# RWKV-7 decays of a head pair: from token-major products to a channel-major product and a scan on VectorE

## What is computed

```
w_log = -softplus(-(w0 + tanh(wl) @ w2)) - 0.5       # wl: 96 low-rank columns of each token
decay = exp(-exp(w_log))                             # one number for each token and channel
S_t   = S_{t-1} * decay_t + (rank-one terms)         # for each token of a sequence, in order
```

## Time and profile before

| | |
|---|---|
| median of 3 runs | 1846.82 us (1845.8 to 1849.24) |
| span of the profiled execution | 1844.8 us, 1.0 us under the fastest run's device time |
| granted TensorE clock, mean | 0.996 |
| TensorE matmul busy | 1811.2 us (98%), weight loads 1733.0 us (94%) |
| VectorE busy | 1132.4 us (61%) |
| ScalarE busy | 729.2 us (40%) |
| chain that ended last | TensorE 94%, VectorE 3%, ScalarE 1%, DMA 1% |
| length of a loop pass | 47.4 us |

### The profile page before, as it was taken

One profiled execution on the slowest core, in us unless ns is written; L12 is line 12 of the kernel. 1 busy time (PEld: TensorE's weight loads), 2 busy tenths in 40 slices (PEclk: granted clock), 3 DMA queues, 4 the chain that ended last, 5 costly groups with the idle time before them and its releaser, 6 DMA issues.

```text
span 1844.8 us, 41091 instructions
## 1 busy us (share of the span) xinstructions
PE 1811.2 (98%) x16688; PEld 1733.0 (94%) x16688; DVE 1132.4 (61%) x2000; ACT 729.2 (40%) x1013; POOL 51.6 (3%) x100
## 2 busy tenths in 40 slices
PE   7999999999999999999999999999999999999997
PEld 6999788888888888899999999999999999999997
DVE  6645675467777777766556666666666665434444
ACT  5433434344444444433444333333333333333332
POOL 0600000000000000000000000000000000000000
PEclk9999999999999999999999999999999999999999
DMA  6644334333333332355446444544445445544443
GB/s 238 223 160 158 108 115 160 119 128 109 107 107 107 107 102 91 130 199 166 167 170 219 160 162 161 177 160 159 161 163 176 159 159 184 188 163 166 161 167 129
DMA packets 50832, 283.52 MB, mean 154 GB/s; under 512 B 7104, under 2 KB 12288, under 8 KB 24656
## 3 DMA queue, kind: packets, MB, share of 16 engines
q1 hardware_dynamic: 43488, 260.80, 41.6%
q10 hardware_dynamic: 3216, 12.82, 1.8%
q0 software_dynamic: 4064, 8.98, 1.5%
HBM read 274.31 MB, written 8.27 MB: 153 GB/s over the span
## 4 chain that ended last, share of the span: by engine, by line
PE 94%; DVE 3%; ACT 1%; DMA 1%; issue 1%; SPq 0%; ACTq 0%; DVEq 0%
PE bank L596 29%; PE bank L598 27%; PE bank L597 27%; PE bank L925 1%; PE bank L960 1%; DVE w_lo L544 1%; PE bank L612 1%; PE bank L1025 0%; PE bank L947 0%; DVE max L1813 0%; PE bank L577 0%; PE bank L725 0%; PE bank L882 0%; PE bank L701 0%; PE bank L791 0%
## 5 line engine op out<-in xcount | busy, mean ns | idle before, releaser
L596 PE MATMUL bank<-x_split,w_lo 128*128 128x288 f32 x2944 | 899.3, 305 | 7.1 <-DVE w_lo L544 6.9
L597 PE MATMUL bank<-x_split,w_hi 128*128 128x288 f32 x2944 | 869.2, 295 | 0.0
L598 PE MATMUL bank<-x_split,w_hi 128*128 128x288 f32 x2944 | 867.0, 294 | 0.0
L560 ACT ACTIVATE w_hi<-w_raw 128x2048 fp32r<-128x2048 f32 (+1 forms) x262 | 468.8, 1790 | 590.4 <-PE bank L598 571.7
L544 DVE TENSOR_TENSOR w_lo<-w_raw,w_hi 128x2048 fp32r<-128x2048 f32 (+1 forms) x238 | 503.6, 2116 | 283.8 <-ACT w_hi L560 283.5
L596 PEld LDWEIGHTS bank<-x_split,w_lo 128*128 128x128 f32 x2944 | 552.4, 188 | 32.1 <-issue 13.6
L597 PEld LDWEIGHTS bank<-x_split,w_hi 128*128 128x128 f32 x2944 | 553.8, 188 | 3.1 <-issue 0.7
L598 PEld LDWEIGHTS bank<-x_split,w_hi 128*128 128x128 f32 x2944 | 554.9, 188 | 0.0
L596 PE MATMUL bank<-act_split,w_lo 128*128 128x288 f32 x704 | 208.6, 296 | 0.0
L597 PE MATMUL bank<-act_split,w_hi 128*128 128x288 f32 x704 | 207.7, 295 | 0.0
L598 PE MATMUL bank<-act_split,w_hi 128*128 128x288 f32 x704 | 207.0, 294 | 0.0
(11 more groups left out here) (384 smaller groups left out, 1499.9 us busy)
## 6 DMA issues: line engine op xcount, KB each, us to landing
w_raw<-in_w_up SPq DMA_DIRECT2D x88, 1024.0 KB, 4.8
w_raw<-in_w_in SPq DMA_DIRECT2D x48, 1024.0 KB, 5.0
w_raw<-in_w_down SPq DMA_DIRECT2D x64, 704.0 KB, 4.1
w_raw<-in_w_gate SPq DMA_DIRECT2D x32, 1024.0 KB, 4.9
w_raw<-in_w_p SPq DMA_DIRECT2D x16, 1024.0 KB, 4.9
w_raw<-in_w_o SPq DMA_DIRECT2D x16, 1024.0 KB, 4.8
x_raw<-in_x SPq DMA_DIRECT2D x4, 576.0 KB, 5.7
h<-in_x ACTq DMA_DIRECT2D x1, 2304.0 KB, 11.1
```

The costliest lines, as they stand in the source:

```text
L560: actv(WHI[:, slot, 0:kt], WRAW[:, slot, 0:kt], ACT.Copy).then_inc(sem("w_hi"), 3 if isinstance(n, int) and n == 2 else 1)
L596: mm(out, wl, hi, start=first and k == ks[0], stop=False, skip_group_check=True)
L597: mm(out, w, lo, start=False, stop=False, skip_group_check=True)
L598: ins = mm(out, w, hi, start=False, stop=last and k == ks[-1], skip_group_check=True)
```

## The change

On TensorE the three token-major products for z become one product with the 128 channels stationary and all 288 tokens moving, so that z has the channels on the partitions at once; `log_decay` (three products and its waits) is gone from TensorE. On ScalarE tanh and the addition of 1 write the tile `log_decays`, 300 columns, in which a zero column stands ahead of each chunk. On VectorE one instruction, `tensor_tensor_scan` over 300 columns, makes the running sums in place: it multiplies the running value by a constant tile that is 0 at the head of each chunk and 1 elsewhere, and adds the next column. It stands between the first two quarters of a split and `k_mixed`. The exps read this tile from SBUF and carry the scale that the triangular constant held. The constants grow from 144 to 104 columns in one tile and from 130 to 300 in the other, 130 columns more together. VectorE clears the new tile once, ahead of the loop.

```diff
-    tri = np.zeros((P, 2, CH + 1))
-    tri[:, :, 1:] = ((blk(CH) & upi) * (0.5 * DECAY_SCALE)).reshape(P, 2, CH)
-    c["tri"] = tri.reshape(P, -1)
+    keep = np.ones((P, DEC))
+    keep[:, 0:NCH * (CH + 1):CH + 1] = 0.0
+    keep[:, NCH * (CH + 1):DEC:DS + 1] = 0.0
+    c["scan_keep"] = keep
...
-    LDT = m("decay_tok", [P, 3, P])
+    LDS = m("log_decays", [P, DEC])
+    ldv = LDS[:, 0:NCH * (CH + 1)].rearrange("p (c f) -> p c f", f=CH + 1)
+    ldv_s = LDS[:, NCH * (CH + 1):DEC].rearrange("p (b f) -> p b f", f=DS + 1)
...
                 lw = COLS[:, T_LW]
-                for tt in range(2):
-                    mm(BK[2][:, tt * P:(tt + 1) * P], lw[0:97, tt * P:(tt + 1) * P], LORA[0:97, 0, :], start=True, stop=True)
-                mm(BK[2][0:NS, 2 * P:3 * P], lw[0:97, SEQ:N], LORA[0:97, 0, :], start=True,
-                   stop=True).then_inc(sem("z_mm"), 1)
+                mm(BK[2][:, 0:N], LORA[0:LORA_W + 1, 0, :], lw[0:LORA_W + 1, 0:N], start=True, stop=True).then_inc(sem("z_mm"), 1)
...
-            def log_decay(v):
-
-                pe.wait_ge(sem("decay_tok"), v)
-                pe.wait_ge(sem("g_sb"), v)
-                for tt in range(2):
-                    w = 2 * (CH + 1)
-                    mm(BK[7][:, tt * w:(tt + 1) * w], LDT[:, tt, :], tri, start=True, stop=True)
-                mm(BK[7][:, NCH * (CH + 1):DEC], LDT[0:NS, 2, :], tri_s, start=True, stop=True).then_inc(sem("log_decay"), 1)
...
                 mm(BK[5][:, 0:N], head_ones, YQ[:], start=True, stop=True).then_inc(sem("y_var"), 1)
-                if not last:
-                    log_decay(it + 2)
                 fill(6)
...
             fill_cols(FILL_DECAY)
-            log_decay(1)
             fill_cols(FILL_BONUS)
...
                 act.wait_ge(sem("z_mm"), v)
-                actv(LDT[:, 0:2, :].rearrange("p t f -> p (t f)"), BK[2][:, 0:2 * P], ACT.Tanh, scale=0.5)
-                actv(LDT[0:NS, 2, :], BK[2][0:NS, 2 * P:3 * P], ACT.Tanh, scale=0.5).then_inc(sem("z_tanh"), 1)
+                actv(ldv[:, :, 1:], BK[2][:, 0:SEQ].rearrange("p (c f) -> p c f", f=CH), ACT.Tanh, scale=0.5)
+                actv(ldv_s[:, :, 1:], by_request(BK[2][:, SEQ:N]), ACT.Tanh, scale=0.5).then_inc(sem("z_tanh"), 1)
...
-                actv(LDT[:, 0:2, :], LDT[:, 0:2, :], ACT.Copy, bias=1.0)
-                actv(LDT[0:NS, 2, :], LDT[0:NS, 2, :], ACT.Copy, bias=1.0).then_inc(sem("decay_tok"), 1)
+                actv(ldv[:, :, 1:], ldv[:, :, 1:], ACT.Copy, bias=1.0)
+                actv(ldv_s[:, :, 1:], ldv_s[:, :, 1:], ACT.Copy, bias=1.0).then_inc(sem("decay_tok"), 1)
...
                 act.wait_ge(sem("log_decay"), v)
-                actv(PEXP[:, 0, :], BK[7][:, 0:DEC], ACT.Exp)
-                actv(PEXP[:, 1, :], BK[7][:, 0:DEC], ACT.Exp, scale=-1.0).then_inc(sem("decay"), 1)
+                actv(PEXP[:, 0, :], LDS[:], ACT.Exp, scale=0.5 * DECAY_SCALE)
+                actv(PEXP[:, 1, :], LDS[:], ACT.Exp, scale=-0.5 * DECAY_SCALE).then_inc(sem("decay"), 1)
...
+            V.memset(LDS[:], 0.0)
...
+            def log_decay(v):
+
+                dve.wait_ge(sem("decay_tok"), v)
+                V.tensor_tensor_scan(LDS[:], scan_keep, LDS[:], 0.0, ALU.mult, ALU.add).then_inc(sem("log_decay"), 1)
...
                 for part in range(2):
                     split_part(dve, n + 3, 1, part)
                 if not last:
+                    log_decay(it + 2)
                     k_mixed(it + 2)
...
             kk_max(1)
+            log_decay(1)
             k_mixed(1)
```

More of the change, by code:

```diff
@@ L114, in constants @@
     b4 = blk(DS)
-    small = np.zeros((P, 3 * NS + DB * (DS + 1) + DB))
+    small = np.zeros((P, 3 * NS + DB))
     both = slice(0, 2 * NS)
@@ L119, in constants @@
     small[s, 2 * NS:3 * NS] = (b4 & low)[s, s]
-    for b in range(DB):
-        small[s, 3 * NS + 5 * b + 1:3 * NS + 5 * b + 5] = (b4 & upi)[s, DS * b:DS * b + DS] * (0.5 * DECAY_SCALE)
-    small[both, 3 * NS + 5 * DB:] = np.arange(2 * NS)[:, None] % NS // DS == np.arange(DB)[None, :]
+    small[both, 3 * NS:] = np.arange(2 * NS)[:, None] % NS // DS == np.arange(DB)[None, :]
     c["small"] = small
@@ L430, in build @@
     mean_ones = MEANS[:]
-    tri = cst("tri")
+    scan_keep = cst("scan_keep")
     eye_ch, m_ab, eye_bl, m16u, m32u = (cst(x) for x in ("eye_ch", "m_ab", "eye_bl", "m16u", "m32u"))
@@ L435, in build @@
     ms_ab, ms_l = small[:, 0:2 * NS], small[:, 2 * NS:3 * NS]
-    tri_s = small[:, 3 * NS:3 * NS + 5 * DB]
-    ms_req = cst("small", 2 * NS)[:, 3 * NS + 5 * DB:3 * NS + 6 * DB]
+    ms_req = cst("small", 2 * NS)[:, 3 * NS:3 * NS + DB]
     h_spill = nc.dram_tensor("h_spill", [P, KT * N], F32, kind="Internal").ap()
@@ L1417, in kk_root_and_decays @@
                 d0 = NCH * (CH + 1)
-                actv(PC[:, 0:NCH], BK[7][:, CH:d0:CH + 1], ACT.Exp)
-                actv(PC[:, NCH:], BK[7][:, d0 + DS:DEC:DS + 1], ACT.Exp).then_inc(sem("chunk_decay"), 1)
+                actv(PC[:, 0:NCH], LDS[:, CH:d0:CH + 1], ACT.Exp, scale=0.5 * DECAY_SCALE)
+                actv(PC[:, NCH:], LDS[:, d0 + DS:DEC:DS + 1], ACT.Exp, scale=0.5 * DECAY_SCALE).then_inc(sem("chunk_decay"), 1)
             def mix_cur(it, v):
```

## The result

The changed kernel took 1863.03 us (median of 4 runs, 1862.72 to 1864.65) against 1846.71 (1845.8 to 1849.24) for the kernel before: a ratio of **1.0095 [1.0083, 1.0107]**. The forecast was 1845.3, with 1850.0 as the upper end. The kernel became 0.9% slower, by 16.3 us.

A forecast was written before the change was run, and what follows sets the result against it. TensorE and VectorE were both taken as critical in each pass's second half, with 0.03 us slack. Seven crossings (-0.7) and the pre-loop (-0.84) gave -1.5 us, from 1846.8 to 1845.3, range 1839.5 to 1850.0.

The forecast's parts named there:

- Part 4: Work taken as hidden: exps, SBUF reads and ScalarE patterns off the path; clearing and more constants cost nothing.
- The "slower" rival: Dear scan in VectorE's tied stretch: 0.2% slower at 1.35 us; at 2.04 us +9.2, 1856.0; chance 0.12.
- z in one product: TensorE's z products, ahead of the mean of y and ahead of the loop: 0.50 us saved in each place.
- The rival that this saves little: One z product takes as long as the three it replaces: +2.5 us, 1849.3; chance 0.09.
- The scan: On VectorE ahead of k_mixed: 0.70 us for 300 columns, multiply and add counted one after the other.
- Both waits: VectorE's waits for ScalarE before k_mixed and before the reciprocal: the scan eats both, 0.27 us, leaving VectorE 0.43 late.
- The cheap and the dear scan: Scan rivals on VectorE: at 0.38 us, -4.1 us, chance 0.14; at 2.04 us, +9.2 us, chance 0.12.
- Slack 0.03: Second half of each pass: TensorE's L925 could start at 460.27 after VectorE's L2019, starts at 460.30; both engines critical.
- TensorE waits 1.39: After the mean of y TensorE is 0.99 early, VectorE 0.43 late, slack 0.03: the 0.99 is given back.
- The sum in a pass: Each of seven crossings from pass to pass: -0.50 + 0.43 - 0.03 = -0.10 us, -0.7 in seven.
- The pre-loop: Ahead of the loop TensorE saves 1.49 us, waits 0.65 for a split, and 0.84 is left.
- TensorE alone decides: Rival: VectorE's slack is larger than read, so all TensorE savings count, 8 x 1.49 = 11.9 us, 1834.9; chance 0.11.

The follow-up runs named there:

- The four versions that only lose the halts: Changed kernel with 21 empty increments ahead, head pinned to slot 16, 8 empty increments, or a back-edge prefetch hint: 1843.14, 1845.10, 1846.45, 1848.45 us.
- experiment 6: Changed kernel with head pinned to slot 16, plus three unused float32 products put back on TensorE where the decay sums stood: 1846.57 us, passes 47.20.
- the hint: Changed kernel with a branch prefetch hint on the pair loop's back edge on TensorE, one instruction more at the head: 1848.45 us, ratio 1.0003.

## Why the prediction was wrong

**The step that failed.** None of the terms that it gave a price: what failed is that the sum had only these. Part 4 ("what is hidden") counted clearing, constants and ScalarE's patterns and put everything else at nothing without a reason. TensorE's instructions were counted for their time and never for their place. The change makes TensorE's code 21 instructions shorter ahead of the loop and its body 21 shorter; that moves the head from slot 13 to slot 248, and though the body is shorter, it now touches eight blocks in place of seven. Price: two halts and a slow clock, 8.1 us, at each of two of the six branches back, 16.3 us together, where the sum had 0. This was no rival either. The "slower" rival was a dear scan, and its own sign (a scan record over 1.2 us) did not come. It could have been asked before: the page of the kernel before has a row for the queue that brings instructions, and that the engine's program gets shorter could be counted from the diff.

**z in one product: right.** TensorE's timeline in the changed kernel, the pair of rows in the loop and the same ahead of it:

```profile
437.09 0.75 PE L825 MATMUL bank<-cols,lora 97*128 97x288 f32 x2
...
438.16 0.65 PE L831 MATMUL bank<-cols,lora 128*128 128x288 f32 x2
```

```profile
381.12 0.65 PE L825 MATMUL bank<-cols,lora 97*128 97x288 f32 x2
...
382.09 0.65 PE L831 MATMUL bank<-cols,lora 128*128 128x288 f32 x2
```

438.16 - 437.09 = 1.07 and 382.09 - 381.12 = 0.97, the forecast in both places, against 1.57 and 1.47. The rival that this saves little is out.

**The scan: right, 0.69 for 0.70.** VectorE in the first pass of the changed kernel:

```profile
439.41 0.46 DVE L2117 SCALAR_TENSOR_TENSOR y<-bank,y 128x288 f32<-128x288 f32 x1 [0.96 <-PE bank L1074]
...
440.20 1.28 DVE L552 TENSOR_TENSOR w_lo<-w_raw,w_hi 128x512 fp32r<-128x512 f32 x2
441.40 0.77 DVE L1922 TENSOR_TENSOR_SCAN log_decays<-main_consts,log_decays 128x300 f32<-128x300 f32 x1
442.09 0.43 DVE L1938 SCALAR_TENSOR_TENSOR k_mixed<-k_mixed,rkv 128x288 f32<-128x288 f32 x1
...
444.19 1.94 DVE L1950 RECIPROCAL squares_k<-squares_k 128x288 f32<-128x288 f32 x1
```

The record is 0.77, start to start 0.69, twice what an elementwise operation of that size takes (0.38 by the working of the earlier trace rows); the half rate of the Trainium skill (DVE: opcode table, instruction layouts, handler registers and perf-mode slots, section 6) holds. Both waits were eaten: the scan starts where the quarters end, the reciprocal too. It starts 444.19 - 438.65 = 5.54 after the y-mean product, against 443.83 - 438.69 = 5.14: **0.40 late** for 0.43. The cheap and the dear scan are out.

**Slack 0.03, and TensorE waits 1.39: right.** TensorE's second half of the pass:

```profile
444.33 0.40 PE L596 MATMUL bank<-x_split,w_lo 128*128 128x288 f32 x1 [0.47 <-DVE w_lo L552]
```

```profile
451.76 0.40 PE L596 MATMUL bank<-x_split,w_lo 128*128 128x288 f32 x1 [0.29 <-DVE w_lo L544]
...
460.63 0.58 PE L913 MATMUL bank<-u_and_t,l 32*32 32x64 f32 x26
```

and the work of VectorE that the last row needs:

```profile
460.21 0.27 DVE L2010 TENSOR_TENSOR u_and_t<-u_and_t,bank 128x128 f32<-128x128 f32 x1
```

460.21 + 0.27 + 0.14 = 460.62, and L913 starts at 460.63. Against the y-mean product it stands 21.98 later, 21.61 before the change: 0.37 late, where without a tie it would be 0.99 early. So TensorE waits 1.36 in that half. The table of waits shows only 0.76 of it (0.47 + 0.29). The rest lies in the rounds of small products, where no row names a wait, as none did before the change. The three places are those named: the start of the pass's last unit (its quarters, L552, now stand behind the scan), `fill(2)`, and the first L913 rounds.

**The sum in a pass: -0.16 for -0.10** (47.37 to 47.21), and the interval into the last pass +0.27: that pass makes no next pair, so nothing of the 0.50 comes back in it, while the tie ahead of it is paid. The saving in z of the first crossing lies ahead of the first interval. Together -0.50 - 6 x 0.16 + 0.27 = -1.2 for -0.7.

**The pre-loop: -0.95 for -0.84.** From its first z product to the unit it is 389.95 - 381.12 = 8.83, against 390.00 - 380.22 = 9.78; TensorE waited there 0.36, not 0.65:

```profile
389.95 0.40 PE L596 MATMUL bank<-x_split,w_lo 128*128 128x288 f32 x1 [0.36 <-DVE w_lo L544]
```

The sum of the parts is then -1.2 - 0.95 = -2.1 us, for -1.5. The four versions that only lose the halts and were run ten times each have ratios of 0.9982, 0.9992, 0.9998 and 1.0003, 0.9994 in the mean, or -1.2 us; three of the four intervals hold 1, so it is the passes, not the medians, that show the gain. "TensorE alone decides" (-11.9 us) is out: experiment 6 shows it directly. On the engine that is busiest over the run (weight loads 94%) 0.99 us of work more or less in each pass changed nothing. So the rule of the Trainium skill (Perfetto Trace Analysis, section Identifying the Most-Contended Engine), to relieve the busiest engine first, misleads here when it is read over the whole run. Read over the stretch it points right: from 440.23 to 460.13 of the kernel before, VectorE is busy 19.11 of 19.90 us (96%) and TensorE's weight loads 18.72 (94%).

## What to carry to other kernels

When an edit changes the number of TensorE's instructions in or ahead of a long hardware loop, count the blocks of 256 that the loop's body touches, before and after: here one block too many cost 8 us in a halted pass, fifty times the 0.16 that the edit was worth in it. Other engines were not tried. The signs are idle time with the releaser "issue" at the branch back, more packets on the instruction queue, and passes of unequal length with equal work. So look at the length of every pass before explaining the median, and pin the head before comparing two versions, or their difference is that of their places.
And an engine at 60% busy can be critical in one stretch: take two dependent instructions there and add up what stands between them. Work taken off that stretch paid nearly in full (47.21 to 46.12 here); work taken off the busiest engine beside it pays nothing.

## What the runs showed of the hardware that was not expected

- TensorE's loop body of seven blocks of 256 instructions runs without a halt (passes 47.2, q8 at 47 or 48 packets). One that reaches 9 to 23 instructions into an eighth halts at every branch back: 6.8 to 7.5 us in one (head in slot 255), or 1.2 to 1.7 us at the branch and then 3.7 to 4.6 (slot 248), or 1.3 to 1.7 and then 3.3 to 3.9 behind the head's products (slot 239). With the head in slot 248 and 2 instructions in the eighth it is 3.15 + 2.97 us, at two branches of six. The Trainium skill (Runtime: NRT & Kernel Launch, section Instruction fetch mechanics) gives the blocks, the sequential prefetch, and for TensorE 2048 instructions, which is eight blocks; these runs agree with that. It also speaks of a window of two pages, and by that a body of seven would have halted at every branch; here the measurement decides.
- What may lie behind it (argued, no run shows what is held): eight blocks fit, and the block behind the body is fetched too. Seven and one fit; with eight, that fetch puts out the head's block, and from there the whole body comes again. The nine packets for each halted branch fit this, and so does the hint, with which the same eight blocks needed none.
- A halt of 3 to 7 us cost the clock too, and so did a wait of 1.6 or 1.7 us at the loop's start (0.57 and 0.62 granted in the next 4 us), where waits of 0.85 and 1.27 us left it at 1.00. With the head one instruction from the block's end, the granted clock in the pause, behind it, and then:

```profile
447.60:454.80 7.20, 0.00 (x0) 0.00 (x0) 3.82 (x6) 2.21 (x2) 0.00 (x0) 0.74 0.43 148
454.80:460.00 5.20, 5.18 (x105) 4.81 (x105) 0.60 (x4) 1.09 (x2) 0.00 (x0) 0.70 0.02 3
460.00:464.00 4.00, 4.00 (x86) 3.54 (x85) 3.73 (x14) 2.48 (x10) 0.00 (x0) 1.00 0.02 4
```

- 235 increments of a semaphore ahead of TensorE's first product moved it from 11.74 to 37.34 us: at most 37.34 / 235 = 0.16 us each, and at least 25.6 / 235 = 0.11, since they ran in part under a wait. The y-mean product came 23.1 us later.
- Open: why the changed kernel itself halts at two of its six branches and passes the other four without one packet on q8, while three other eight-block versions halt at all six. It has 2 instructions in its eighth block, those have 9, 14 and 23; no run varied that alone. Open too is why the wait at the loop's start is 0.8 us in one version and 1.7 in another with equal passes.
